# Score batches that fill two PSUM banks per map in a hybrid attention layer

## What is computed

```python
u = jnp.einsum('bsd,de->bse', rmsnorm(x, norm_pre_g), w_in)
dq, dk, dv, dg, mq, mk, mv, mg = jnp.split(u, splits, axis=-1)
# 4 differential heads: two maps of width 64 each, values of width 128
p = jax.nn.softmax(q @ k.T * scale + bias, axis=-1)      # causal, both maps
w = p[:, :, 0] - lam * p[:, :, 1]
a = rmsnorm(w @ v, subln_g) * (1.0 - lambda_init) * jax.nn.silu(dg)
# 8 block-sparse heads; with 512 tokens and blocks of 256 all past blocks are taken
b = (jax.nn.softmax(q @ k.T * scale + bias, axis=-1) @ v) * jax.nn.silu(mg)
y = jnp.concatenate([a, b], axis=-1) @ w_out
return x + rmsnorm(y, norm_post_g)
```

## Time and profile before

| what | value |
|---|---|
| timed runs | 260.27, 261.77, 262.55 us; median 261.77 us |
| the profiled execution | 260.2 us, of which the span (first to last instruction) 258.4 us |
| TensorE busy | 248.5 us (96%) |
| VectorE busy | 177.7 us (69%) |
| ScalarE busy | 144.4 us (56%) |
| GpSimd busy | 29.4 us (11%) |
| granted TensorE clock | 0.997 of full speed over the span |

### The profile page before, as it was taken

The page is one execution under the profiler, slowest core; times in us unless marked ns, Lnnn a source line. Parts: engine busy times, 40 slices in busy tenths (PEclk is TensorE's granted clock), DMA queues, the critical chain, the costliest instruction groups (busy, mean ns, idle before and its releaser), DMA issues.

```text
span 258.4 us, 4447 instructions
## 1 busy us (share of the span) xinstructions
PE 248.5 (96%) x1605; PEld 124.8 (48%) x1605; DVE 177.7 (69%) x384; ACT 144.4 (56%) x337; POOL 29.4 (11%) x77
## 2 busy tenths in 40 slices
PE   6899999999999999999999999999999999999990
PEld 6555344444544444545455444444444444555570
DVE  2785984349757788798678676976698886935313
ACT  3974872345654666785475685675645675711110
POOL 2156000000000050050004024000000000111101
PEclk9999999999999999999999999999999999999998
DMA  6994785496515334843432755689907639999422
GB/s 225 380 354 134 269 290 178 133 377 178 115 30 127 96 105 107 209 115 103 124 89 65 173 135 149 145 165 183 168 12 147 128 61 182 225 193 258 122 84 82
DMA packets 55402, 41.42 MB, mean 160 GB/s; under 512 B 41536, under 2 KB 41800, under 8 KB 55380
## 3 DMA queue, kind: packets, MB, share of 16 engines
q1 hardware_dynamic: 55380, 41.14, 61.0%
HBM read 29.04 MB, written 2.13 MB: 121 GB/s over the span
## 4 chain that ended last, share of the span: by engine, by line
PE 90%; DVE 3%; DMA 3%; ACT 1%; issue 1%; POOL 0%; SPq 0%; DVEq 0%; POOLq 0%; ACTq 0%
PE unit_ps L524 76%; PE score_ps L543 6%; PE o_ps L563 5%; DMA stage<-in_w_in_dram 3%; PE score_ps L612 1%; PE unit_ps L612 1%; DVE w_lo L774 1%; DVE w_lo L776 1%; PE score_ps L485 1%; ACT junk L635 1%; DVE area L832 0%; ACT area L681 0%; DVE arena L826 0%; DVE area L919 0%; ACT w_hi L649 0%
## 5 line engine op out<-in xcount | busy, mean ns | idle before, releaser
L524 PE MATMUL unit_ps<-w_hi,area 128*128 128x512 f16 x256 | 80.8, 380 | 1.6 <-DVE w_lo L776 0.8
L524 PE MATMUL unit_ps<-area,w_hi 128*128 128x512 f16 x256 | 76.3, 380 | 0.0
L689 ACT ACTIVATE arena<-arena,negmax 128x512 f32<-128x512 f32 (+3 forms) x64 | 35.4, 553 | 49.3 <-DVE negmax L846 49.0
L524 PE MATMUL unit_ps<-area,w_lo 128*128 128x512 f16 x128 | 48.6, 379 | 0.0
L524 PE MATMUL unit_ps<-w_lo,area 128*128 128x512 f16 x128 | 48.6, 379 | 0.0
L524 PEld LDWEIGHTS unit_ps<-w_hi,area 128*128 128x128 f16 x256 | 25.0, 98 | 32.2 <-issue 2.0
L524 PEld LDWEIGHTS unit_ps<-area,w_hi 128*128 128x128 f16 x256 | 23.8, 98 | 26.5 <-issue 0.8
L846 DVE CUSTOM_DVE_ANT_0 arena<-score_ps,strips 128x512 f32<-128x512 f32 (+3 forms) x64 | 28.6, 485 | 8.2 <-PE score_ps L543 8.2
L774 DVE SCALAR_TENSOR_TENSOR w_lo<-stage,g_cols,w_hi 128x512 f16<-128x512 f32 x32 | 24.1, 754 | 9.3 <-ACT w_hi L649 9.3
L776 DVE SCALAR_TENSOR_TENSOR w_lo<-stage,g_cols,w_hi 128x512 f16<-128x512 f32 x32 | 24.8, 776 | 0.0
L648 ACT ACTIVATE w_hi<-stage,g_cols 128x512 f16<-128x512 f32 x32 | 22.7, 711 | 3.3 <-DMA stage<-in_w_in_dram 3.2
(11 more groups left out here) (92 smaller groups left out, 311.8 us busy)
## 6 DMA issues: line engine op xcount, KB each, us to landing
stage<-in_w_in_dram SPq DMA_DIRECT2D x32, 512.0 KB, 4.4
stage<-in_w_out_dram SPq DMA_DIRECT2D x8, 512.0 KB, 3.9
arena<-in_x_dram SPq DMA_DIRECT2D x4, 512.0 KB, 8.2
strips<-bias_rows SPq DMA_DIRECT2D x1, 2048.0 KB, 8.9
stage<-in_x_dram SPq DMA_DIRECT2D x4, 512.0 KB, 4.5
out_dram<-area SPq DMA_DIRECT2D x3, 512.0 KB, 4.6
strips<-bias_rows SPq DMA_DIRECT2D x1, 1024.0 KB, 5.4
g_row<-in_norm_post_g_dram SPq DMA_DIRECT2D x1, 512.0 KB, 10.3
```

Source lines behind the costliest of these rows:

```text
L524: last = nc.tensor.matmul(bank, a, b, start=(k == 0 and n == 0), stop=(k == KT - 1 and n == 2))
L689: nc.scalar.activation(probs[:, i % 2, m, 0:n], probs[:, i % 2, m, 0:n], ACT.Exp, bias=negmax[:, i, m:m + 1], scale=-1.0, accum_out=sums[: ...
```

## The change

The 32 steps are put into 12 batches of one to six steps in place of 16 of two. A batch may fill two banks for each map, and stands at the slot of its first step: slots 0, 3, 6, 8, 11, 14, 16, 22, 25, 27, 29 and 31, in place of all even slots to 30. `score_places` packs the steps of a batch into banks, the widest first: banks 0 and 1 for the first map, 2 and 3 for the second. TensorE now waits once for each batch, for the logits of all earlier steps, and `score_ready` is raised once for each batch, by its last matmul; `logits(i)` waits for the whole batch that holds step i. No matmul, vector or scalar instruction and no DMA is added or removed.

```diff
+    BATCHES = [[0, 1, 2], [3, 4, 5], [6, 7], [8, 9, 10], [11, 12, 13], [14, 15], [16, 17, 18, 19, 20, 21],
+               [22, 23, 24], [25, 26], [27, 28], [29, 30], [31]]
...
+    def score_places():
+
+        where = {}
+        for batch in BATCHES:
+            free = [BANK] * 4
+            for i in sorted(batch, key=lambda i: -STEPS[i][1]):
+                n = (STEPS[i][1] + 1) * P
+                for m in range(2):
+                    bank = next(b for b in (2 * m, 2 * m + 1) if free[b] >= n)
+                    where[i, m] = (bank, BANK - free[bank])
+                    free[bank] -= n
+        return where
...
-                if i >= 2:
-                    pe.wait_ge(logits_ready, 2 * (i - 1))
+                if i in BATCH_AT and i > 0:
+                    pe.wait_ge(logits_ready, 2 * i)
...
-                last.then_inc(score_ready, 1)
+                if i == BATCH_OF[i][-1]:
+                    last.then_inc(score_ready, 1)
...
-                if j < NSTEP and j % 2 == 0:
-                    scores(j)
-                    scores(j + 1)
+                for i in BATCH_AT.get(j, ()):
+                    scores(i)
...
-                dve.wait_ge(score_ready, i + 1)
+                dve.wait_ge(score_ready, BATCHES.index(BATCH_OF[i]) + 1)
```

More of the change, by code:

```diff
@@ L124, in x_count @@
         return sum(X_PARTS[:t]) + part + 1
+    BANK = 512
+    BATCHES = [[0, 1, 2], [3, 4, 5], [6, 7], [8, 9, 10], [11, 12, 13], [14, 15], [16, 17, 18, 19, 20, 21],
+               [22, 23, 24], [25, 26], [27, 28], [29, 30], [31]]
+    BATCH_AT = {batch[0]: batch for batch in BATCHES}
+    BATCH_OF = {i: batch for batch in BATCHES for i in batch}
+    def score_places():
[9 more added lines that the diff above has]
+        return where
+    SCORE_AT = score_places()
     def place(i):
@@ L542, in scores @@
                         part = slice(m * DH, (m + 1) * DH)
-                        last = nc.tensor.matmul(score_ps[:, 2 * (i % 2) + m, 0:n], a[part, ch, rows], b[part, ch, 0:n],
+                        bank, col = SCORE_AT[i, m]
+                        last = nc.tensor.matmul(score_ps[:, bank, col:col + n], a[part, ch, rows], b[part, ch, 0:n],
                                                 start=first, stop=final)
-                last.then_inc(score_ready, 1)
+                if i == BATCH_OF[i][-1]:
+                    last.then_inc(score_ready, 1)
             def values(i):
@@ L845, in logits @@
                     h = c if r == 0 else DIFF_HEADS + 2 * c + m
-                    nc.vector.tensor_tensor_reduce(out=probs[:, i % 2, m, 0:n], in0=score_ps[:, 2 * (i % 2) + m, 0:n],
+                    bank, col = SCORE_AT[i, m]
+                    nc.vector.tensor_tensor_reduce(out=probs[:, i % 2, m, 0:n], in0=score_ps[:, bank, col:col + n],
                                                    in1=strips[:, h, 0:n][:, ::-1], scale=-1.0, scalar=-MASKED,
```

## The result

The changed kernel takes 262.83 us in the median of 17 runs (261.13 to 265.21), the kernel before 261.0 us (17 runs, 259.69 to 262.99). The ratio is 1.0074, with a 95% interval of 1.0052 to 1.0095: slower by 1.9 us (1.4 to 2.5). The forecast was a change of +2.6 us, 263.6 us with a range of 260.6 to 265.6. The measured change lies inside the 1% that the forecast held likeliest, though it is clearly above zero. The longest of the 17 runs after, 265.21 us, is in a slower state that some executions show; without it the median is 262.76 us. The profiled execution of the changed kernel has a span of 262.4 us at a clock of 0.995.

The account below looks back on a forecast made before the run. TensorE was taken to bound the kernel, busy 248.5 of 258.4 us. Terms -0.80 + 1.17 + 1.0 + 1.25 = +2.6 us took the profiled 260.2 to 262.8, with half the distance to the median 263.6 us, range 260.6 to 265.6.

Parts of the forecast that it names:

- the 1% that the forecast held likeliest: Whole kernel: time within 1% (2.6 us) of the kernel before, given 61%, against slower 36% and faster 3%.
- The gain of 0.8 us: TensorE score batches: each costs 0.20 us in changes between 128 and 64 rows, so four fewer save 0.8 us.
- The rival of a full drain each way: TensorE array changes: each costs 0.16 us and not 0.10, all sums 0.5 lower; chance 4%.
- Term 1, values(0): Attention start: logits(0) waits for steps 1 and 2, 0.65 us, so step 0's tile lands late; +1.17 us.
- Term 2, values(28): Slot 30: step 28's transpose goes out 0.87 us later, lands 5.3 later, and TensorE waits 1.0 us.
- Term 3, values(31): Attention end: step 31's scores come 3.3 us later, its transpose lands late, and TensorE waits 1.1 to 1.6 us.
- The sum: Whole kernel: the batch saving and three waits, -0.80 + 1.17 + 1.0 + 1.25 = +2.6 us.
- The middle: Batches of slots 3, 11 and 25: they hold VectorE up but cost nothing; uncovered, one would cost 1.0 us.
- The level: Forecast median: profiled execution 262.8 us plus half of the 1.57 us between it and the runs' median, 263.6 us.

Follow-up runs that it names:

- e5_apart: Kernel before with one filler quarter between the two steps of every batch from slot 2 on, fifteen batches more: ratio 1.0122, +3.2 us.
- e8_first: Kernel before with only its first batches changed to [0, 1, 2] and [3], still sixteen batches: ratio 1.0065, +1.7 us.
- e2_start: Changed kernel with first batch [0, 1, 2] cut into [0, 1] and [2], thirteen batches: ratio 1.0048, +1.3 us against the kernel before.
- e3_end: Changed kernel with last batches [29, 30], [31] made [29], [30, 31], still twelve: ratio 1.0014, +0.4 us against the kernel before.
- e12_early: Changed kernel with the signal raised once no later step of the batch shares a bank with the steps done: 1.0055, +1.4 us against the kernel before.
- e7_last: Kernel before with step 31 alone in a batch at slot 31, seventeen batches: ratio 1.0072, +1.9 us.
- e6_xlate: Changed kernel with the third and fourth loads of x a slot later, third behind step 31's transpose: 1.0007, +0.2 us against the kernel before.
- e1_pairs: Changed kernel with sixteen batches of two steps, keeping one wait and one signal per batch: ratio 1.0004, +0.1 us against the kernel before.
- e4_both: Changed kernel with first batch cut into [0, 1], [2] and last made [29], [30, 31], thirteen batches: 0.9997, -0.1 us against the kernel before.
- e10_best: Kernel before with twelve batches keeping its first and last, third and fourth x loads a slot later, early signals: 260.51 us against 261.31, ratio 0.9968.
- e11_before_xlate: Kernel before with the third and fourth loads of x a slot later: ratio 1.0000, 0.0 us.

## Why the prediction was right, and where it was not

**The gain of 0.8 us: right.** A batch of the changed kernel still shows 0.31 us in and 0.10 over the pitch out (54.87 to 55.18 and 56.33 to 56.59 in slot 0, where a pair of 384 columns needs 0.16), as in the earlier trace rows, and e5_apart measured 0.21 us a batch. The rival of a full drain each way, at 0.33 us a batch, fell with it. The Trainium skill (TensorEngine Tiling (Array Packing), Key Properties) says that a change of the mode drains the engine; the rows show a cost at each change, as that rule has it, but less than the 0.16 us that the prediction took for a drain. That figure came from the 0.38 us with which a matmul is shown, an end that the profile models, so whether the array is empty at a change is not shown.

**Term 1, values(0): right.** The delay of logits(0) was put at 0.65 us and was 0.64; values(0) started 0.73 later, against +0.65, as its tile took 3.7 us to land where the earlier trace rows had 3.6. The wait was 67.21 - 65.44 - 0.22 = 1.55 us, 1.28 more than before, against 1.17. e8_first shows that the start alone makes the kernel slower. e2_start took 0.6 us out of the changed kernel where 1.0 was expected, since half a microsecond of the added wait stays there.

**Term 2, values(28): wrong.** The step that failed is "lands 5.3 later at 218.8". TensorE arrived as forecast (d = -0.44 against -0.49). The transpose went out 0.62 us later than before (214.82 - 55.18 = 159.64, against 212.64 - 53.62 = 159.02) rather than 0.87, but it landed in 4.2 us and not 5.3. The landing is what decided: with 5.3 TensorE would have waited 0.7 us. I had taken the longer landing of one execution as a property of the transpose. Over the profiled kernels this one landing was between 4.2 and 5.8 us. The distance to the load of x behind it does not sort them (at 2.0 to 2.1 us both 4.3 and 5.8 occur), and what does is open. TensorE waited for this tile by 0.10 us in e3_end and 0.24 in e12_early and nowhere else, so the term belonged in the sum with a fraction of its 1.0 us.

**Term 3, values(31): right in kind, under-sized.** Put at 1.1 to 1.6 us, it was 238.79 - 236.52 - 0.22 = 2.05. Since TensorE did not wait at values(28), slot 31 began sooner than I had it, the scores of step 31 came 2.4 and not 3.3 us later, and SyncE issued the transpose 2.25 later, 0.8 sooner than the middle of the forecast. But TensorE came to values(31) 0.93 sooner than forecast (d = +0.43 against +1.36), the landing was 6.4 and not 6.0, and values(31) started 0.14 behind the landing, which I had left out here. These make up the distance from 1.35, the middle of the range, to 2.05. The explanation rests on the timed runs of e7_last, e3_end and e6_xlate: with the load in front the late scores cost, and without either of the two the cost is gone. In single traces the load in front and scores in time can give a wait as well (1.24 us in e1_pairs).

**The sum.** -0.80 + 1.28 + 0 + 2.05 = +2.5 us against the trace's +2.44; the forecast had -0.80 + 1.17 + 1.0 + 1.25 = +2.6. Two errors of about 1 us cancelled. That the total came out is therefore luck in part. The runs say +1.9 (1.4 to 2.5); the trace's 2.44 is at the upper edge of that, and e1_pairs shows how far a trace can be off, with 1.2 us in its trace against 0.1 in its runs.

**The middle: right.** Batches at slots 3, 11 and 25 held VectorE up and cost nothing: VectorE's waits for scores rose (the page has 13.9 us of idle time in front of the logits for 8.2 before), TensorE's did not: in the changed kernel's trace it waits at values(0) and values(31) and nowhere between. e4_both and e10_best bear it out. **The level** of 263.6 was 0.8 too high, and not for its base: half of the distance between the profile and the median put the kernel before at 260.2 + 0.8 = 261.0, and 261.0 is what its 17 runs gave. All of the 0.8 is the change, +1.8 between the medians where +2.6 was forecast, so the waits added up in the sum were too long by that.

## What to carry to other kernels

When work on the bounding engine is grouped to save a fixed cost per group, price also what the new places of the group do to its consumers: the first and the last step had almost no slack here from which a delay could be paid (0.14 and 0.31 us from landing to use). Signal a part of a group when its consumer can start, not the group as a whole; here that brought the first use back by 0.66 us in the trace, though the timed runs do not tell the gain from zero. Where a late transfer is on the path, look at what stands in front of it in its queue; moving that was worth as much here as undoing the late work.

## What the runs showed that I had not expected

- The last transpose landed after 6.0 to 6.6 us in the eleven profiled kernels in which the load of x was issued directly in front of it (6.0 before, 6.4 after), and after 5.1 to 5.3 us in the three in which it was not (e6_xlate, e10_best, e11_before_xlate). The load costs the transpose behind it about 1.1 us (6.2 against 5.2 in the mean), beside the 0.66 us in which it holds up the issue. All of it is in the issue, which took 3.8 to 4.5 us against 3.1 to 3.2; from the end of the issue to the landing it is 1.8 to 2.2 us either way.
- The same transpose of step 28 landed after 5.3 us before and 4.3 us with pairs, where all engines have the same work in the same order.
- At values(31) the kernel before started 0.3 us after the landing in its trace, and the kernel with pairs waited 1.1 us in its own, while timed runs of the two agree (ratio 1.0004, 0.9983 to 1.0025). Reserves of that size in one trace are not reserves.
